# Local attention: three of eight output projection tiles accumulated pair by pair inside the attention, with scores in four PSUM banks and turns and outputs in two

## The reference

```python
def odd_layer_mixer(h, hc, w_qkv, w_out, sink, rope, need_ctx):
    p = h @ w_qkv                     # 16 query heads, 4 key/value heads, of 64
    ...
    def block(n):                     # 128 queries at a time
        ...
        return _sink_attend(qb, [(kc, vc, None), (kb, vb, valid)], sink_logit)
    o = lax.map(block, jnp.arange(nb))
    y = jnp.moveaxis(o, 0, 1).reshape(b_, t_, d_) @ w_out
```

## Time and profile before

| what | value |
|---|---|
| median of three runs | 2216.28 us (2216.21 to 2219.28) |
| the profiled execution: its span | 2215.9 us |
| the profiled execution's own time, measured around it | not given; the median lies 0.4 us above the span |
| TensorE busy | 2067.2 us, 93% |
| VectorE busy | 711.9 us, 32% |
| ScalarE busy | 400.4 us, 18% |
| attention, first scores to end of the last output | 1157.5 to 1223.0 us |
| projection, first matmul to last residual's start | 1223.5 to 1251.4 us |
| second stage of experts, first weight matmul | 1278.8 us |

### The profile page before, as it was taken

How to read it: one execution, slowest core, us unless ns; L and a number is a source line. 1 busy time by engine, 2 the same in 40 slices (tenths; PEclk the granted TensorE clock), 3 DMA queues, 4 the chain that set the end, 5 groups by cost and what they waited for, 6 DMA issues and landing times. The chain is left out here.

```text
span 2215.9 us, 25873 instructions
## 1 busy us (share of the span) xinstructions
PE 2067.2 (93%) x10204; PEld 1109.1 (50%) x10204; DVE 711.9 (32%) x1712; ACT 400.4 (18%) x866; POOL 56.4 (3%) x79
## 2 busy tenths in 40 slices
PE   5999999996999999999798799999999899898999
PEld 2345546753334334334374633333333776576887
DVE  3034218724211110111538211111111598721411
ACT  2014200012100110110217211111111232421100
POOL 0000000001000000000100200000000000000000
PEclk8999999997999999999899999999999999898999
DMA  9661119412799999999820589999999722233240
GB/s 360 248 237 39 53 61 342 169 39 92 311 428 428 401 429 428 393 428 416 321 107 8 197 342 427 429 428 428 427 428 422 289 98 97 105 114 132 77 152 20
DMA packets 115417, 573.33 MB, mean 259 GB/s; under 512 B 6288, under 2 KB 20880, under 8 KB 90752
## 3 DMA queue, kind: packets, MB, share of 16 engines
q1 hardware_dynamic: 105440, 539.28, 60.7%
q0 software_dynamic: 7296, 27.29, 3.3%
q10 hardware_dynamic: 2592, 5.51, 0.6%
HBM read 563.41 MB, written 8.65 MB: 258 GB/s over the span
## 5 line engine op out<-in xcount | busy, mean ns | idle before, releaser
L525 PE MATMUL banks<-pages,weight_ring 128*128 128x256 f32 (+1 forms) x1984 | 522.8, 425 | 8.4 <-ACT pages L1625 3.2
L525 PEld LDWEIGHTS banks<-pages,weight_ring 128*128 128x128 f32 x1984 | 381.1, 193 | 149.2 <-issue 100.8
L991 PE MATMUL banks<-weight_ring,pages 128*64 128x512 f32 x976 | 220.0, 597 | 6.8 <-DMA weight_ring<-in_moe_w_gate 2.8
L1937 DVE TENSOR_TENSOR pages<-banks,pages 128x512 f32<-128x512 f32 (+3 forms) x173 | 98.9, 611 | 359.8 <-PE banks L899 179.3
L1710 ACT ACTIVATE pages<-banks 128x512 f32<-128x512 f32 (+1 forms) x150 | 84.4, 572 | 682.7 <-PE banks L871 116.0
L929 PE MATMUL banks<-weight_ring,pages 128*64 128x512 f32 x832 | 184.1, 598 | 3.2 <-issue 3.2
L1937 DVE TENSOR_TENSOR pages<-pages 128x512 f32<-128x512 f32 (+9 forms) x298 | 173.7, 604 | 11.9 <-ACT pages L1815 2.6
L1600 ACT ACTIVATE pages<-banks 128x256 f32<-128x256 f32 (+2 forms) x188 | 76.6, 433 | 546.0 <-PE banks L525 340.3
L1937 DVE TENSOR_TENSOR pages<-pages,banks 128x512 f32<-128x512 f32 (+1 forms) x41 | 28.2, 688 | 408.1 <-PE banks L991 176.8
L991 PEld LDWEIGHTS banks<-weight_ring,pages 128*64 128x64 f32 x976 | 68.4, 138 | 151.7 <-issue 134.5
L1101 PE MATMUL banks<-weight_ring,pages 128*64 128x512 f32 x512 | 114.3, 596 | 6.4 <-DVE pages L2394 5.4
(11 more groups left out here) (312 smaller groups left out, 1911.6 us busy)
## 6 DMA issues: line engine op xcount, KB each, us to landing
weight_ring<-in_moe_w_down SPq DMA_DIRECT2D x64, 2048.0 KB, 17.0
weight_ring<-in_moe_w_up SPq DMA_DIRECT2D x63, 2048.0 KB, 17.9
weight_ring<-in_moe_w_gate SPq DMA_DIRECT2D x62, 2048.0 KB, 16.5
weight_ring<-in_ada_w SPq DMA_DIRECT2D x24, 2048.0 KB, 15.8
weight_ring<-in_even_w_in SPq DMA_DIRECT2D x18, 2048.0 KB, 19.8
weight_ring<-in_odd_w_in SPq DMA_DIRECT2D x8, 2048.0 KB, 7.5
weight_ring<-in_odd_w_out SPq DMA_DIRECT2D x6, 2048.0 KB, 8.9
weight_ring<-in_odd_w_qkv SPq DMA_DIRECT2D x3, 2048.0 KB, 13.0
```

Source lines behind the costliest of these rows:

```text
L525: last = pe.matmul(b[:, 0:w], s[:, k, m * P:(m + 1) * P], src(k)[:, t0:t0 + w], start=(k == 0), stop=(k == nk - 1))
L991: last = pe.matmul(to, xg[:, par, k, 64 * half:64 * half + 64], rows, start=(half == 0 and k == 0), stop=(half == 1 and k == 3))
L1937: return dve.tensor_tensor(out_, a, b, op)
```

## The change

The attention's jobs get fixed banks: scores the banks 0 to 3 in turn, the turns of head `m` bank `4 + m`, the outputs bank 5. The tiles 0, 1 and 2 of weight block `outc` 0 get banks 6 (both halves) and 7, and stay open over the whole attention. A new function `outc_added(j)` adds pair `j`'s share to the three tiles: three matmuls. The loop becomes one iteration longer. TensorE in iteration `i`: scores of `i`; in even iterations from 4 on the output of pair `(i - 4) // 2`, now ahead of the turn; the turn of `i - 1`; in odd iterations from 5 on `outc_added((i - 5) // 2)`. The last pair's addition follows the loop, and then `project` makes the remaining five tiles. ScalarE's evacuation of an output moves ahead of the exponentials in its iteration. VectorE waits for the three tiles at once, and its residual takes tile 1 from the upper half of its bank.

```diff
--- before.py
+++ after.py
@@ -273,6 +273,7 @@
     vC = pages(5, 1024, 1024).rearrange("p (s n) -> p s n", s=4)
     yC = pages(6).rearrange("p (j t) -> p j t", j=8)
     window = pages(10, 1024).rearrange("p (b k) -> p b k", b=2)
+    OUTC_AT = ((6, 0), (6, 256), (7, 0))
     dup = pages(10, 256, 1024).rearrange("p (a m) -> p a m", a=2)
     sink_up = pages(10, 16, 1280)
     kD = pages(12).rearrange("p (a t) -> p a t", a=4)
@@ -513,11 +514,11 @@
                     last = pe.matmul(b[:, hd * P:(hd + 1) * P], row_to_all(j, hd), R, start=True, stop=True)
                 close_job(job, last)
 
-        def project(stage, name, src, nk, tiles, w, t0=0, n=512, norm=None, per_k=1, after=None):
+        def project(stage, name, src, nk, tiles, w, t0=0, n=512, norm=None, per_k=1, after=None, first=0):
 
             wait_weights(pe, name)
             s = slot(name, nk, n)
-            for m in range(tiles):
+            for m in range(first, tiles):
                 b = open_job((stage, name, m))
                 for k in range(nk):
                     if norm and m == 0:
@@ -1173,7 +1174,7 @@
             j, qt = unitsC[i]
             for m in range(2):
                 job = ("cs", i, m)
-                b = open_job(job)
+                b = open_job(job, (2 * i + m) % 4)
                 close_job(job, pe.matmul(b, qC[64 * m:64 * m + 64, j, qt * P:(qt + 1) * P],
                                          kD[64 * m:64 * m + 64, j // 2], start=True, stop=True))
 
@@ -1182,7 +1183,7 @@
                 pe.wait_ge(sem("sink_diag"), 2 * i + m + 1)
                 wait_taken(pe, ("cs", i, m))
                 job = ("ct", i, m)
-                b = open_job(job)
+                b = open_job(job, 4 + m)
                 n = (2 * i + m) % 4
                 for kk in range(4):
                     last = pe.transpose(b[:, kk * P:(kk + 1) * P], probsC[:, n, kk * P:(kk + 1) * P], ident)
@@ -1196,7 +1197,7 @@
             if j == 0:
                 for s in range(4):
                     wait_taken(pe, ("m2v", ("qkv", 0, 2), s))
-            b = open_job(job)
+            b = open_job(job, 5)
             kv = j // 2
             for s in range(4):
                 for m in range(2):
@@ -1204,17 +1205,35 @@
                                      start=(s == 0), stop=(s == 3))
             close_job(job, last)
 
-        for i in range(len(unitsC) + 2):
+        def outc_added(j):
+
+            name = ("outc", 0, 0)
+            wait_taken(pe, ("co", j))
+            if j == 0:
+                wait_weights(pe, name)
+                for m, (bk, at) in enumerate(OUTC_AT):
+                    open_job(("m2o", name, m), bk) if at == 0 else next_in_bank(("m2o", name, m), bk)
+            s = slot(name, KT, 512)
+            for m, (bk, at) in enumerate(OUTC_AT):
+                last = pe.matmul(banks_mem[:, bk, at:at + NX], s[:, j, m * P:(m + 1) * P], yC[:, j],
+                                 start=(j == 0 and at == 0), stop=(j == KT - 1 and m > 0))
+                if j == KT - 1:
+                    close_job(("m2o", name, m), last)
+
+        for i in range(len(unitsC) + 3):
             if i < len(unitsC):
                 sink_scores(i)
+            if i >= 4 and i % 2 == 0:
+                sink_out((i - 4) // 2)
             if 1 <= i <= len(unitsC):
                 sink_turn(i - 1)
-            if i >= 3 and i % 2 == 1:
-                sink_out((i - 3) // 2)
-        for j in (6, 7):
-            wait_taken(pe, ("co", j))
-        for c in range(2):
-            project("m2o", ("outc", 0, c), lambda k: yC[:, k], KT, 4, NX)
+            if i >= 5 and i % 2 == 1:
+                outc_added((i - 5) // 2)
+        outc_added(7)
+        in_banks(0, 1, 2, 3, 4, 5)
+        project("m2o", ("outc", 0, 0), lambda k: yC[:, k], KT, 4, NX, first=3)
+        project("m2o", ("outc", 0, 1), lambda k: yC[:, k], KT, 4, NX)
+        in_banks(*range(8))
         experts(1, 2)
 
 
@@ -1801,6 +1820,9 @@
             for m in range(4):
                 evac(("m2", ("qkv", 0, c), m), qC[:, 4 * c + m], NX)
         for i in range(19):
+            if i >= 4 and i % 2 == 0:
+                j = (i - 4) // 2
+                evac(("co", j), yC[:, j], NX)
             if i < 16:
                 j = i // 2
                 for m in range(2):
@@ -1814,9 +1836,6 @@
                                    accum_out=statC[:, n, 3:4]).then_inc(taken_sem(("cs", i, m)), 1)
                     act.activation(statC[:, n, 4:5], statC[:, n, 2:3], ACT.Exp, bias=vec("sink", head, 1))\
                         .then_inc(sem("sink_exp"), 1)
-            if i >= 4 and i % 2 == 0:
-                j = (i - 4) // 2
-                evac(("co", j), yC[:, j], NX)
             if 1 <= i <= 16:
                 j, qt = (i - 1) // 2, (i - 1) % 2
                 for m in range(2):
@@ -1962,9 +1981,9 @@
             dve.wait_ge(sem("norm_scaled"), norm_before(stage) + KT * (w // NX))
             dve.sem_inc(taken_sem((stage, "spread")), 1)
 
-        def residual(job, k, l, j, halves):
-
-            b = result(dve, job)
+        def residual(job, k, l, j, halves, at=0):
+
+            b = result(dve, job)[:, at:512]
             for s in range(halves):
                 sl = slice(s * NX, (s + 1) * NX)
                 last = dve.scalar_tensor_tensor(X[:, k, sl], b[:, sl], mod[:, l, j + k, s:s + 1], X[:, k, sl],
@@ -2475,9 +2494,10 @@
                     link(tt(st[:, 5:6], st[:, 3:4], st[:, 4:5], ALU.add))
                     link(dve.reciprocal(st[:, 6:7], st[:, 5:6]))
                     dve.tensor_scalar(probsC[:, n], probsC[:, n], st[:, 6:7], None, ALU.mult).then_inc(sem("sink_diag"), 1)
+        result(dve, ("m2o", ("outc", 0, 0), 1))
         for c in range(2):
             for m in range(4):
-                residual(("m2o", ("outc", 0, c), m), 4 * c + m, 1, 16, 1)
+                residual(("m2o", ("outc", 0, c), m), 4 * c + m, 1, 16, 1, OUTC_AT[m][1] if c == 0 and m < 3 else 0)
         link(tt(gain_sq, vec("fin_g"), vec("fin_g"), ALU.mult))
         link(tt(vec("pre", 0, 8), vec("pre", 0, 8), vec("fin_g"), ALU.mult))
         experts(1, 2)
```

## The result

The changed kernel takes 1.0016 of the time of the kernel before (95% interval 1.0009 to 1.0024), over 12 runs of each: medians 2221.38 and 2218.03 us. That is 3.5 us slower, 2.0 to 5.3 by the interval. The forecast was 2.8 us slower.

What follows compares the result with a forecast made beforehand. The prediction took VectorE and ScalarE's exponential to bound the attention, with full transfers bounding the second expert stage. 2215.9 + 8.8 + 3.05 - 9.07 = 2218.7, plus 0.4: 2219.1 us; range 2212.5 to 2223.0, the forecast's own 2218 to 2221.3.

Steps and rivals of the forecast that it cites:

- The pace: Local attention: VectorE and ScalarE's exponential form a gapless loop, 3.785 us a unit; a late exponential delays everything one for one.
- The wait for bank 5: Even units made late by an output (penalised): output waits for ScalarE's turn copy, 5.25 us instead of 3.785, six times.
- E: Start of a unit's first exponential on ScalarE in the attention; turn copies were put as done at E + 2.85.
- rival 1: Attention: bank wait covered, exponential at 4.45 us, total 2213.4, or 2209.4 if that lateness is absorbed too; chance 0.15.
- The odd unit: Attention: the odd unit keeps 3.785 us, so a pair takes 9.04 us and six pairs lose 8.8 us.
- Rival 2: Attention: TensorE's clock falls to half, 5.8 us more a pair; two pairs give 2230.7, all six 2253.9; chance 0.11.
- Loop in sum: Attention loop: six outputs ahead of exponentials cost 1.465 us each, 8.8 us lost.
- The end and the gain: After the last exponential: 3.05 us lost at the attention's end, 9.07 us gained as three tiles leave the projection tail.
- The sum: Whole kernel: 2215.9 + 8.8 + 3.05 - 9.07 = 2218.7, with 0.4 us added 2219.1 us.
- Added matmuls at nothing: Attention: three added matmuls a pair, 1.3 us on TensorE, cost nothing; unhidden weight loads would be 0.62 us each.
- the lower ends: Low side of the chain's terms (0.04, 0.26, output 1.95): 6 x 1.33 + 2.85 - 9.1 = +1.7 us.
- Shift passed through whole: Second expert stage: transfers are full and weight refill follows the first expert, so an earlier or later start reaches the end whole.

Runs made afterwards that it cites:

- Experiment 3: Changed kernel with outputs in bank 3, scores in three banks, and the output's evacuation back behind the exponentials; ratio 0.9965 of the kernel before.
- Experiment 1: Changed kernel with outputs in a bank of their own (bank 3) and scores in three banks, same order of work; ratio 0.9972 of the kernel before.
- experiment 5: Changed kernel with twelve unused identity transposes into bank 7 in each of iterations 2, 3 and 4; ratio 1.0018 of the kernel before.
- experiment 7: Changed kernel with a fourth tile added in the upper half of bank 7, four matmuls a pair; ratio 0.9999 of the kernel before.
- experiment 4: Changed kernel's banks and order with nothing added in the attention, all eight tiles made after the loop; ratio 1.0070 of the kernel before.
- experiment 9: Outputs in their own bank, after the turn, evacuated behind the turn copies; four tiles added instead of three; ratio 0.9943 of the kernel before.
- experiment 8: Changed kernel reordered: outputs in their own bank, after the turn, evacuated behind the turn copies; three tiles added; ratio 0.9963 of the kernel before.
- experiment 6: Changed kernel run once more, unmodified, for its profile; one timed execution 2223.85 us, stage 97.11 us.

## Why the prediction was right, step by step

The mechanism was right: the wait for bank 5 and the early evacuation set the pace, and each measured link of the chain is near the one forecast. The nearness of the sum is helped by luck: the odd unit cost less than forecast, and a fall of the clock that the sum did not have cost more.

- *The pace.* VectorE and the exponential form the loop, and a late exponential delays one for one: right. Experiment 3 has pairs of 7.57 with more work on TensorE.
- *The wait for bank 5, 5.25 us a penalised unit:* measured 5.25, and each of its terms: copies to E + 2.84, 0.15, 1.98, 0.28. That 0.15 is the middle of a bracket of 0.04 to 0.25, a choice that turned out well. Experiment 1 takes away the bank's sharing alone and gets 4.40 (rival 1 had priced the same case at 4.45).
- *The odd unit* was said to keep 3.785. It is 3.72. In the changed kernel the second exponential follows a late first one by 0.85 us (1186.74, then 1187.59) instead of 0.91; that its input had been ready for long is my reading, which no run tests. So six pairs cost 6 x 1.40 = 8.4 us and not 8.8 (the last one 0.1 more).
- *The clock.* Rival 2 was priced as all or nothing, two pairs or six; the forecast's own sum had zero for it. By the prediction's own list, a granted clock below 1.00 in the attention was a sign of this rival, and it came. But its price did not: the profile has one fall, at the first output, for 0.9 us, and not 5.8 us for each slow pair. This is the term that was mis-sized. The rival named the right place for it (idle time lumped before an output), and the first of these lumps stands where nothing is added yet. The profile of experiment 5, which fills it, is 0.9 us shorter; the profile of experiment 7, which does not, has no fall either. So the fall is likely there with the gap, but that the gap alone decides it is not shown. The Trainium skill, page "TensorE: Matmul & The Clock Gate", section "A second HAM failure mode: psum-queue depth-cycling", says that small idle gaps between groups of matmuls that cycle through PSUM banks can make the clock swing between its levels and cost throughput. The trace of the changed kernel agrees at the gap of 2.10 us before the first output, and not at the six later ones (five of 0.79 us and one of 1.85), where the clock held 1.00.
- *Loop in sum:* last exponential 68.59 us after the first scores, before 59.14: 9.45 lost (8.4 in the pairs, 0.9 with the clock, 0.1 in the last pair), forecast 8.8.
- *The end and the gain:* +3.05 and -9.07 were forecast, -6.02 together; measured 28.66 - 34.76 = -6.10.
- *The sum:* 9.45 - 6.10 = 3.35 us; forecast 2.8; by the timed runs 3.5.
- *Added matmuls at nothing:* right. Experiments 4 and 7 leave the units the same with none and with four. The 0.62 us for a matmul with its weight loads not hidden is worked out from no row; it did not occur, the three take 1.46 us together.
- *Two slips without effect:* the lower ends give 2.85 + 0.04 + 1.95 + 0.26 - 3.785 = 1.315 a pair and not 1.33; and the rows have 1251.43 - 1223.53 = 27.9 us from the projection's start to the last residual, not 27.4, and correspondingly 1255.12 - 1236.25 = 18.9 after the change, not 18.6.
- *Shift passed through whole:* the refill came 3.58 later with 0.34 of it from before the attention; the remainder of the program varies by up to 4 us from profile to profile. Which stages those are I did not test. Against the kernel before, the timed difference of the runs follows that of the stage within 0.1 to 2.8 us (largest in experiment 9), so the shift passes through in the main.

## What to carry to other kernels

When accumulation tiles take PSUM banks for a long time, the question is not how many banks each kind of job gets, but whose release each job now waits for: follow the previous user of the bank to the engine that frees it, and see where in that engine's order the release stands. Here scores got four banks that three could have served, and the output shared one with a turn; other bank numbers and nothing else turned a loss of 3.5 us into a gain of 6.2 us. Then put the evacuation where its engine idles, not ahead of work on the loop, and fill the busiest engine up to the loop's pace. Slightly beyond it can still pay: in experiment 9 the fourth tile made each pair 0.1 us longer than in experiment 8, 0.5 us in the loop, and took 2.6 us off the tail.

## What the runs showed of the hardware that was not expected

TensorE's granted clock fell inside the attention in nine of the twelve profiles (not in that of the kernel before, of experiment 5 and of experiment 9), also far from any output: between 1161 and 1168 in experiment 1 and between 1159 and 1163 in experiment 7, when the loop did not wait for TensorE. One program can have such a fall and not have it: the changed kernel held 1.00 from 1159 to 1163 in its first profile, and in its second (experiment 6) had 0.50 from 1161 on. So one profile does not settle whether a fall belongs to a kernel. These early falls cost nothing (units of 3.78 us as elsewhere); the same level under the first output cost 0.9 us, and in experiment 4 the one at a unit of 6.10 us cost 0.85. The profile shows the fall, but only the units' distances show whether it was on the path.
